# The low parts of a streamed weight matrix: all on VectorE, in quarters, and none on GpSimd in the second pass

## The chip, the cores and the metric

The kernel runs on one core of one Trainium2 chip. The metric is device time in microseconds (us). TensorE multiplies matrices, VectorE (DVE in the rows) and ScalarE (ACT) work element by element on 128 partitions, GpSimd (POOL) can do the same and issues the indirect DMAs here, and SyncE (SP) issues the plain DMAs. Each engine runs its own instructions in order and waits for others by semaphores. PE is TensorE's matmul, PEld its weight load.

## The reference

One decoder layer for 512 prompt tokens and 32 sample tokens (544 columns). What matters here is its last part, a channel mixer of 16384 single-neuron experts with a dense expansion in the kernel:

```
xt = rms_norm(h)                                   # n tokens x 1024
s1, s2 = scores of xt @ w_query against keys1, keys2      # 8 heads, 128 + 128 keys
top, idx = the 16 best of the 256 sums of the 16 best of each  # per token and head
g   = softmax(top)
act = gelu(einsum('nd,nhkd->nhk', xt, expert_u[idx]))
out = einsum('nhk,nhkd->nd', g * act, expert_v[idx])
```

`expert_u` and `expert_v` are 16384 x 1024 in fp32, 64 MB each. All is fp32. The kernel makes each product of fp32 operands from three products of parts: a high part (a rounded copy) and a low part (the rest, value minus high part).

## The kernel before, in words

The mixer runs over `expert_u` twice. A step is 256 of the 16384 experts (`STEPS` = 64 steps, a 1 MB piece of u and one of v each).

**Pass one** (steps 0 to 63) computes the activations of tokens 0 to 255 for every expert and stores them to device memory (`acts_sparse`). **Pass two** (steps 64 to 127 of u, each followed four steps later by its v piece) does the 288 other tokens densely: activations times gates, then the product with v. In the same pass the first 256 tokens get their output sparsely: for each of 256 (token tile, slot) pairs k, GpSimd fetches one activation per partition (`fetch_unit`, L651) and one 4 KB row of v per partition (`fetch_row`, L658), and VectorE adds row times share into an accumulator in PSUM (`add_row`, L1428). Six row buffers (`RING`) stand between the two: the fetch of row k+6 waits until row k is used.

**A slot** of pass two is one round of the loop `for slot in range(ENDS)` that every engine has. From slot 4 on TensorE does `up` for step 64+slot (48 matmuls of 288 columns, two halves j of 24), then `down` for v piece slot-4 (48 matmuls, two halves o). ScalarE rounds the next u piece (`high_u`, L924) and the next v piece (`high_v`, L969), applies gelu (L954), and rounds the activations (L976). VectorE does, in this order: the second half of the last `down` is added (`add_block`, L1458), `split_u` of the next step (L1451), about two rows, `gate_acts` (two L1470), `split_v` (L1485), `low_acts` (two L1479), the first half of this `down` is added (L1458), and about two rows. SyncE loads the next pieces when a low part has freed their buffer.

**Low parts of u.** `on_vector(t)` says who makes the low part of step t: in pass one GpSimd always; in pass two VectorE, but of the steps from 69 on every third (t = 69, 72, ... 126: 20 steps) GpSimd. GpSimd's `split_u` (L646) is two instructions of 1024 elements, each telling `u_lo_pool`. It stands in GpSimd's row of work between the first and second half of the slot's fetches. `wait_low_u` makes TensorE wait for whichever engine has the step. VectorE's `split_u` and `split_v` are one instruction of 2048 elements each. The low part of v is always VectorE's.

In pass one GpSimd does the 64 low parts of u, and that of step 64, as two instructions each.

Of the kernel before, what the change touches and what calls it, by code (L numbers as in the profile page):

```python
# [93 lines left out]

def on_vector(t):

    return t > STEPS and (t <= STEPS + BESIDE or t % 3 != 0)


def splits_until(t):  # L100
# [5 lines left out]
def u_buffer(t):  # L106

    return t % 3 if t < STEPS else 1 - t % 2
# [24 lines left out]
def rows_added_at(slot):  # L133

    return range(rows_until(slot), rows_until(slot + 1))
# [29 lines left out]
def build_layer(nc, io):  # L165
# [134 lines left out]
    def by_blocks(ap):  # L300

        return ap.rearrange("p (k c) -> p k c", k=KD)
# [176 lines left out]
    with nc.Block() as block:  # L479
# [118 lines left out]
        def _(pool):  # L598
# [42 lines left out]
            def split_u(t):  # L641
                pool.wait_ge(u_hi_done, t + 1)
                w = t % 2 if t < STEPS else place_of_u(t - STEPS)
                for j in range(2):
                    cols = slice(P * j, P * (j + 1))
                    pool.tensor_tensor(lows[w][:, :, cols], by_blocks(u_raw[u_buffer(t)])[:, :, cols],  # L646
                                       highs[w][:, :, cols].bitcast(F32), ALU.subtract).then_inc(u_lo_pool, 1)

            def fetch_unit(k):

# [28 lines left out]
            for slot in range(ENDS):  # L679
                for k in range(PIECE * slot, PIECE * slot + PIECE):  # L680
                    if k < AHEAD:
                        fetch_unit(k)
                mine = rows_added_at(slot)
                for k in mine[:len(mine) // 2]:
                    fetch_ahead(k)
                if slot + 1 < STEPS and not on_vector(STEPS + slot + 1):
                    split_u(STEPS + slot + 1)
                for k in mine[len(mine) // 2:]:
                    fetch_ahead(k)

        @block.scalar
# [323 lines left out]
        def _(v):  # L1015
# [432 lines left out]
            def split_u(t):  # L1448
                w = place_of_u(t - STEPS)
                v.wait_ge(u_hi_done, t + 1)  # L1450
                v.tensor_tensor(lows[w], by_blocks(u_raw[u_buffer(t)]), highs[w].bitcast(F32), ALU.subtract)\  # L1451
                    .then_inc(u_lo_vector, 2)

            def add_block(c, o):

# [26 lines left out]
            def split_v(c):  # L1482
                w = place_of_v(c)
                v.wait_ge(v_hi_done, c + 1)
                v.tensor_tensor(lows[w], by_blocks(v_raw[c % 2]), highs[w].bitcast(F32),  # L1485
                                ALU.subtract).then_inc(v_lo_done, 1)

            def add_total(tile):

# [491 lines left out]
```

## Time and profile before

| | |
|---|---|
| median of 3 runs | 2034.12 us (2033.16 to 2038.95) |
| the profiled execution | 2026.33 us |
| its span in the trace | 2024.9 us |
| pass two with both products, of the span | 1102 to 1991 us |
| TensorE matmul busy, of the span | 1847.7 us (91%) |
| VectorE, ScalarE, GpSimd busy | 1482.8, 822.7, 1199.6 us |

The profile's page gives shares over the whole program, which has stages with different limits. Pass one and the stages before it end near 1062 us, and the loop with both products, 60 slots, runs from 1102 to 1991 us. A row on a wait names the engine and line that waited and the one that released it. "issue" means that nothing the profile shows released it, and "remote" a releaser that it did not find.

### The profile page before, as it was taken

How to read it: one execution, taken by the hardware profiler on the slowest of the kernel's cores; microseconds unless marked ns; L12 is line 12 of the kernel's file. 1: busy time of each engine (PE TensorE's matmuls, PEld its weight loads, DVE VectorE, ACT ScalarE, POOL GpSimd, SP SyncE). 2: the span in 40 equal slices, each digit the busy share in tenths (PEclk: the TensorE clock that was granted, in tenths of full speed). 3: DMA queues.
4: the chain of work that ended last, by engine and by line, in shares of the span. 5: the costliest groups of instructions: out<-in, count | busy, mean ns of one | idle time of the engine just before them, and what ended most of it. 6: DMA issues, size and time to landing. Idle time of an engine off the chain costs nothing.

```text
span 2024.9 us, 37848 instructions
## 1 busy us (share of the span) xinstructions
PE 1847.7 (91%) x14571; PEld 1740.4 (86%) x14571; DVE 1482.8 (73%) x2584; ACT 822.7 (41%) x1103; POOL 1199.6 (59%) x855
## 2 busy tenths in 40 slices
PE   7988988798999999999997999998988998989798
PEld 6977764368999999999997999898988998989798
DVE  3669665523589889857765787888768788887977
ACT  4233764423214454457673333343333333333332
POOL 3322222232236888855647787878777778787861
PEclk8999999889999999999998999899999998998999
DMA  5434878652125777756778888988878998998875
GB/s 169 74 106 151 289 253 291 220 219 81 63 98 163 222 225 231 226 185 261 268 289 295 279 302 316 323 311 312 301 279 291 330 318 299 319 318 284 291 276 196
DMA packets 207789, 492.19 MB, mean 243 GB/s; under 512 B 34209, under 2 KB 119266, under 8 KB 187138
## 3 DMA queue, kind: packets, MB, share of 16 engines
q1 hardware_dynamic: 145906, 319.11, 46.4%
q0 software_dynamic: 55296, 167.94, 23.0%
q10 hardware_dynamic: 6416, 2.78, 1.0%
q8 instruction: 116, 1.90, 0.4%
q14 instruction: 55, 0.45, 0.1%
HBM read 449.10 MB, written 40.66 MB: 242 GB/s over the span
## 4 chain that ended last, share of the span: by engine, by line
PE 60%; POOL 13%; DVE 11%; issue 6%; ACT 4%; another core or an unknown queue 3%; DVEq 2%; DMA 1%; ACTq 0%; SPq 0%; POOLq 0%
PE pair L1529 16%; PE pair L1531 16%; PE pair L1530 16%; POOL v_rows L658 6%; POOL picked_a L651 6%; PE pair L1862 3%; PE pair L1674 3%; DVE pair L1428 2%; POOL w_lo L646 2%; DVE act L1470 1%; PE pair L1686 1%; DVEq L1422 1%; PE pair L1726 1%; PE pair L1812 1%
## 5 line engine op out<-in xcount | busy, mean ns | idle before, releaser
L1529 PE MATMUL pair<-x_hi,w_hi 128*128 128x256 f32 (+2 forms) x2224 | 664.9, 299 | 78.1 <-POOL w_lo L646 55.4
L1530 PE MATMUL pair<-x_lo,w_hi 128*128 128x256 f32 (+2 forms) x2224 | 653.8, 294 | 0.7 <-issue 0.7
L1531 PE MATMUL pair<-x_hi,w_lo 128*128 128x256 f32 (+2 forms) x2224 | 652.5, 293 | 0.1
L1529 PEld LDWEIGHTS pair<-x_hi,w_hi 128*128 128x128 f32 x2224 | 434.2, 195 | 83.4 <-POOL w_lo L646 58.8
L1530 PEld LDWEIGHTS pair<-x_lo,w_hi 128*128 128x128 f32 x2224 | 433.7, 195 | 1.9 <-issue 1.7
L1531 PEld LDWEIGHTS pair<-x_hi,w_lo 128*128 128x128 f32 x2224 | 431.9, 194 | 0.7 <-issue 0.7
L658 POOL DMA_INDIRECT v_rows<-in_v_t,at_row x256 | 294.5, 1150 | 148.6 <-DVE pair L1428 80.0
L651 POOL DMA_INDIRECT picked_a<-acts_sparse,at_unit x256 | 325.8, 1273 | 80.3 <-issue 74.9
L1428 DVE SCALAR_TENSOR_TENSOR pair<-v_rows,share,pair 128x1024 f32<-128x1024 f32 x254 | 327.5, 1289 | 25.2 <-issue 3.0
L646 POOL TENSOR_TENSOR w_lo<-w_raw,w_hi 128x1024 fp32r<-128x1024 f32 x106 | 253.1, 2410 | 90.6 <-ACT w_hi L924 90.4
L630 POOL TENSOR_TENSOR w_lo<-w_raw,w_hi 128x2048 fp32r<-128x2048 f32 x22 | 101.5, 4614 | 233.9 <-ACT w_hi L715 233.9
L1529 PE MATMUL pair<-a_hi,w_hi 128*128 128x288 f32 x688 | 209.3, 304 | 14.0 <-issue 13.3
L1530 PE MATMUL pair<-a_lo,w_hi 128*128 128x288 f32 x688 | 208.2, 303 | 6.9 <-issue 6.9
L1531 PE MATMUL pair<-a_hi,w_lo 128*128 128x288 f32 x688 | 208.7, 303 | 5.6 <-issue 5.5
L954 ACT ACTIVATE act<-pair 128x288 f32<-128x288 f32 x128 | 52.6, 411 | 365.7 <-PE pair L1531 198.1
L646 POOL TENSOR_TENSOR w_lo<-v_raw,w_hi 128x1024 fp32r<-128x1024 f32 x64 | 151.6, 2392 | 60.5 <-ACT w_hi L924 60.2
L924 ACT ACTIVATE w_hi<-w_raw 128x2048 fp32r<-128x2048 f32 x64 | 122.4, 1912 | 75.4 <-PE pair L1531 39.0
L1529 PEld LDWEIGHTS pair<-a_hi,w_hi 128*128 128x128 f32 x688 | 133.6, 194 | 15.8 <-issue 15.6
L1470 DVE TENSOR_TENSOR act<-act,g_in 128x288 f32<-128x288 f32 x128 | 77.4, 634 | 92.9 <-ACT act L954 67.1
L1530 PEld LDWEIGHTS pair<-a_lo,w_hi 128*128 128x128 f32 x688 | 133.9, 195 | 10.6 <-issue 10.6
L1531 PEld LDWEIGHTS pair<-a_hi,w_lo 128*128 128x128 f32 x688 | 133.7, 194 | 8.7 <-issue 8.5
L954 ACT ACTIVATE act_out<-pair 128x256 f32<-128x256 f32 x128 | 51.2, 401 | 137.8 <-PE pair L1531 126.4
(234 smaller groups left out, 3775.9 us busy)
## 6 DMA issues: line engine op xcount, KB each, us to landing
w_raw<-in_u_t SPq DMA_DIRECT2D x74, 1024.0 KB, 5.3
v_raw<-in_u_t SPq DMA_DIRECT2D x54, 1024.0 KB
w_raw<-in_v_t SPq DMA_DIRECT2D x128, 256.0 KB
v_raw<-in_v_t SPq DMA_DIRECT2D x128, 256.0 KB
gates<-g_out SPq DMA_DIRECT2D x9, 2048.0 KB, 8.6
g_in<-gates SPq DMA_DIRECT2D x16, 1152.0 KB
v_ring<-in_cache_v SPq DMA_DIRECT2D x64, 256.0 KB, 3.8
v_ring<-in_cache_v POOLq DMA_DIRECT2D x64, 256.0 KB, 4.6
```

The costliest lines, as they stand in the source:

```text
L630: pool.tensor_tensor(w_lo[:, chunk % 2, :], w_raw[:, chunk % 2, :], w_hi[:, chunk % 2, :].bitcast(F32), ALU.subtract).then_inc(w_split, 1)
L646: pool.tensor_tensor(lows[w][:, :, cols], by_blocks(u_raw[u_buffer(t)])[:, :, cols], highs[w][:, :, cols].bitcast(F32), ALU.subtract).then ...
L651: pool.indirect_dma_start(picked_a[:, k:k + 1], None, every_unit[:, :], bass.IndirectOffsetOnAxis(ap=at_unit[:, k:k + 1], axis=0))\
L658: pool.indirect_dma_start(v_rows[:, k % RING, :], None, every_row[:, :], bass.IndirectOffsetOnAxis(ap=at_row[:, k:k + 1], axis=0))\
L924: sc.activation(into, by_blocks(u_raw[u_buffer(t)]), ACT.Copy).then_inc(u_hi_done, 1)
L954: sc.activation(kept, made, ACT.Gelu).then_inc(gelu_done, 1)
L1428: v.scalar_tensor_tensor(total, row, share[:, k:k + 1], total, ALU.mult, ALU.add).then_inc(row_used, 1)
L1470: v.tensor_tensor(mine, mine, g_in[:, slot, :, GCHUNK * tile:GCHUNK * (tile + 1)], ALU.mult)\
L1529: te.matmul(out, s_hi, m_hi, start=start, stop=False)
L1530: te.matmul(out, s_hi, m_lo, start=False, stop=False)
L1531: return te.matmul(out, s_lo, m_hi, start=False, stop=stop)
L1674: last = te.transpose(bank(PAGE_TURN[j % 2])[:, P * pr:P * (pr + 1)], pages_in[chunk % 4][:, j, P * pr:P * (pr + 1)], ident[:, :])
```

## The change

`on_vector(t)` is true for every step of pass two, so the 20 low parts that GpSimd made are VectorE's, and GpSimd only fetches there. VectorE's instruction for a low part, of u and of v, is cut into four of 512 elements each, with one semaphore update behind the last. GpSimd's in pass one is cut in two again: four instructions of 512 elements, an update behind each second. GpSimd's loop of pass two keeps its order of fetches and loses the split between them (the `split_u` call stays in the text, but its condition is never true).

```diff
 def on_vector(t):
 
-    return t > STEPS and (t <= STEPS + BESIDE or t % 3 != 0)
+    return t > STEPS
...
                 for j in range(2):
                     cols = slice(P * j, P * (j + 1))
-                    pool.tensor_tensor(lows[w][:, :, cols], by_blocks(u_raw[u_buffer(t)])[:, :, cols],
-                                       highs[w][:, :, cols].bitcast(F32), ALU.subtract).then_inc(u_lo_pool, 1)
+                    for first in (0, KD // 2):
+                        mine = slice(first, first + KD // 2)
+                        last = pool.tensor_tensor(lows[w][:, mine, cols], by_blocks(u_raw[u_buffer(t)])[:, mine, cols],
+                                                  highs[w][:, mine, cols].bitcast(F32), ALU.subtract)
+                    last.then_inc(u_lo_pool, 1)
...
-                mine = rows_added_at(slot)
-                for k in mine[:len(mine) // 2]:
-                    fetch_ahead(k)
                 if slot + 1 < STEPS and not on_vector(STEPS + slot + 1):
                     split_u(STEPS + slot + 1)
-                for k in mine[len(mine) // 2:]:
+                for k in rows_added_at(slot):
                     fetch_ahead(k)
...
             def split_u(t):
                 w = place_of_u(t - STEPS)
                 v.wait_ge(u_hi_done, t + 1)
-                v.tensor_tensor(lows[w], by_blocks(u_raw[u_buffer(t)]), highs[w].bitcast(F32), ALU.subtract)\
-                    .then_inc(u_lo_vector, 2)
+                for q in range(4):
+                    mine = slice(2 * q, 2 * q + 2)
+                    last = v.tensor_tensor(lows[w][:, mine], by_blocks(u_raw[u_buffer(t)])[:, mine],
+                                           highs[w][:, mine].bitcast(F32), ALU.subtract)
+                last.then_inc(u_lo_vector, 2)
...
             def split_v(c):
                 w = place_of_v(c)
                 v.wait_ge(v_hi_done, c + 1)
-                v.tensor_tensor(lows[w], by_blocks(v_raw[c % 2]), highs[w].bitcast(F32),
-                                ALU.subtract).then_inc(v_lo_done, 1)
+                for q in range(4):
+                    mine = slice(2 * q, 2 * q + 2)
+                    last = v.tensor_tensor(lows[w][:, mine], by_blocks(v_raw[c % 2])[:, mine],
+                                           highs[w][:, mine].bitcast(F32), ALU.subtract)
+                last.then_inc(v_lo_done, 1)
```

How the work stands on VectorE before, in slots 4 and 5. Slot 4 has no split of u, slot 5 has one; `w_lo`, `x_lo` are two of the three places of low parts, `pair` is PSUM.

```order
L1428 SCALAR_TENSOR_TENSOR pair<-v_rows,share,pair 128x1024 x3
L1470 TENSOR_TENSOR act_129<-act_129,g_in 128x288 x2
L1485 TENSOR_TENSOR x_lo<-v_raw_119,x_hi 128x8x256
L1479 TENSOR_TENSOR a_lo_128<-act_129,a_hi_127 128x288 x2
L1458 TENSOR_TENSOR resid<-resid,pair 128x288
L1428 SCALAR_TENSOR_TENSOR pair<-v_rows,share,pair 128x1024 x2
L1458 TENSOR_TENSOR resid<-resid,pair 128x288
L1451 TENSOR_TENSOR w_lo<-w_raw,w_hi 128x2048
L1418 TENSOR_TENSOR share<-share,picked_a 128x8
L1428 SCALAR_TENSOR_TENSOR pair<-v_rows,share,pair 128x1024 x2
```

The same place in the changed kernel. The first row here is the last row of slot 3, then comes slot 4's own split of u (L1453, before L1451).

```order
L1428 SCALAR_TENSOR_TENSOR pair<-v_rows,share,pair 128x1024
L1453 TENSOR_TENSOR w_lo<-v_raw_115,w_hi 128x512 x4
L1428 SCALAR_TENSOR_TENSOR pair<-v_rows,share,pair 128x1024 x2
L1473 TENSOR_TENSOR act_129<-act_129,g_in 128x288 x2
L1490 TENSOR_TENSOR x_lo<-v_raw_119,x_hi 128x2x256 x4
L1482 TENSOR_TENSOR a_lo_128<-act_129,a_hi_127 128x288 x2
L1461 TENSOR_TENSOR resid<-resid,pair 128x288
L1428 SCALAR_TENSOR_TENSOR pair<-v_rows,share,pair 128x1024 x2
L1461 TENSOR_TENSOR resid<-resid,pair 128x288
L1453 TENSOR_TENSOR w_lo<-w_raw,w_hi 128x512 x4
```

Every slot now has a split of u, and each split is four instructions. Nothing else on VectorE moved.

GpSimd before, late in pass two, around one of its splits.

```order
L651 DMA picked_a<-acts_sparse,at_unit 128x1
L658 DMA v_rows<-in_v_t,at_row 128x1024
L646 TENSOR_TENSOR w_lo<-w_raw,w_hi 128x8x128 x2
L651 DMA picked_a<-acts_sparse,at_unit 128x1
L658 DMA v_rows<-in_v_t,at_row 128x1024
```

In the changed kernel the row L646 is gone there and the fetches follow each other without a break; from one of the old splits to the next there are 26 fetches, or 13 pairs, in three slots.

## Rows read from the trace of the kernel before

**Rows 1.** The page: busy time, and the span in 40 slices.

```profile
PE 1847.7 (91%) x14571; PEld 1740.4 (86%) x14571; DVE 1482.8 (73%) x2584; ACT 822.7 (41%) x1103; POOL 1199.6 (59%) x855
...
PEclk8999999889999999999998999899999998998999
DMA  5434878652125777756778888988878998998875
```

**Rows 2.** Stretches: us, busy (instructions) per engine, granted clock, DMA share, GB/s.

```profile
1102.00:1991.00 889.00, 805.72 (x5722) 792.72 (x5720) 723.79 (x736) 314.55 (x359) 678.90 (x522) 0.94 0.87 302
...
1573.00:1599.00 26.00, 26.00 (x198) 26.00 (x197) 21.73 (x24) 10.41 (x12) 20.82 (x18) 1.00 1.02 377
1651.00:1690.00 39.00, 38.45 (x290) 38.21 (x288) 37.78 (x41) 16.27 (x19) 28.62 (x23) 1.00 0.87 297
```

**Rows 3.** Waits of TensorE, 1102 to 1991: us in total, times, longest.

```profile
PE pair L1529 <- POOL w_lo L646: 51.9, 10, 8.7
PE pair L1529 <- issue: 14.7, 22, 1.5
PE pair L1530 <- issue: 8.3, 18, 1.0
PE pair L1531 <- issue: 5.9, 13, 1.1
PE pair L1890 <- issue: 2.1, 3, 1.1
```

**Rows 4.** GpSimd in order, 1546 to 1576: start, us, what, [idle before].

```profile
1553.46 1.00 POOL L651 DMA_INDIRECT picked_a<-acts_sparse,at_unit  x1 [0.30 <-issue]
1554.76 2.27 POOL L658 DMA_INDIRECT v_rows<-in_v_t,at_row  x1 [0.30 <-issue]
...
1562.04 4.67 POOL L646 TENSOR_TENSOR w_lo<-v_raw,w_hi 128x1024 fp32r<-128x1024 f32 x2
```

**Rows 5.** VectorE in order, 1546 to 1592.

```profile
1553.92 2.29 DVE L1485 TENSOR_TENSOR x_lo<-v_raw,x_hi 128x2048 fp32r<-128x2048 f32 x1
...
1563.97 4.89 DVE L1451 TENSOR_TENSOR w_lo<-w_raw,w_hi 128x2048 fp32r<-128x2048 f32 x1 [1.64 <-ACT w_hi L924]
...
1578.66 0.45 DVE L1458 TENSOR_TENSOR resid<-resid,pair 128x288 f32<-128x288 f32 x1
...
1588.45 2.29 DVE L1485 TENSOR_TENSOR w_lo<-v_raw,w_hi 128x2048 fp32r<-128x2048 f32 x1 [0.48 <-ACT w_hi L969]
1590.66 0.82 DVE L1479 TENSOR_TENSOR a_lo<-act,a_hi 128x288 fp32r<-128x288 f32 x2
1591.40 0.45 DVE L1458 TENSOR_TENSOR resid<-resid,pair 128x288 f32<-128x288 f32 x1
```

**Rows 6.** Groups by shape, 1102 to 1991: busy, mean ns, idle before.

```profile
L1428 DVE SCALAR_TENSOR_TENSOR pair<-v_rows,share,pair 128x1024 f32<-128x1024 f32 x245 | 315.9, 1289 | 24.0 <-issue 2.5
L651 POOL DMA_INDIRECT picked_a<-acts_sparse,at_unit x236 | 300.0, 1271 | 69.2 <-issue 69.2
L658 POOL DMA_INDIRECT v_rows<-in_v_t,at_row x246 | 283.2, 1151 | 139.2 <-DVE pair L1428 73.6 <-issue 65.4 <-DVE pair L1426 0.3
L1485 DVE TENSOR_TENSOR w_lo<-w_raw,w_hi 128x2048 fp32r<-128x2048 f32 x20 | 45.8, 2292 | 10.5 <-issue 5.4 <-ACT w_hi L969 5.0
```

**Rows 7.** The picks (L651) of the whole program: ns min/median/max.

```profile
L651 POOL DMA_INDIRECT picked_a<-acts_sparse,at_unit x256: 940/945/2990, 1061.9 to 1957.3; - x128
```

**Rows 8.** The low parts on GpSimd: ns min/median/max; one by shape.

```profile
L646 POOL TENSOR_TENSOR w_lo<-v_raw,w_hi x64: 2352/2395/2417, 599.4 to 1923.5; 128x1024 fp32r<-128x1024 f32 x64
L630 POOL TENSOR_TENSOR w_lo<-w_raw,w_hi 128x2048 fp32r<-128x2048 f32 x22 | 101.5, 4614 | 233.9 <-ACT w_hi L715 233.9
```

**Rows 9.** In order, 1590 to 1612: TensorE, ScalarE, GpSimd.

```profile
1598.39 0.30 PE L1529 MATMUL pair<-x_hi 128*128 128x288 f32 x1
1598.52 0.29 PE L1530 MATMUL pair<-x_lo,x_hi 128*128 128x288 f32 x1
1598.65 0.30 PE L1531 MATMUL pair<-x_hi,x_lo 128*128 128x288 f32 x1
1598.78 0.30 PE L1529 MATMUL pair<-a_hi,w_hi 128*128 128x288 f32 x1
...
1604.98 0.41 ACT L954 ACTIVATE act<-pair 128x288 f32<-128x288 f32 x1 [6.81 <-remote]
...
1602.82 4.71 POOL L646 TENSOR_TENSOR w_lo<-w_raw,w_hi 128x1024 fp32r<-128x1024 f32 x2
```

**Rows 10.** Waits in pass one, and in slots 0 to 3.

```profile
PE pair L1529 <- POOL w_lo L646: 3.5, 5, 0.7
...
PE pair L1529 <- DVE w_lo L1451: 6.9, 2, 4.9
```

## The prediction

> **What bounds the kernel now.** I read the page first, then the stretches, then the waits of TensorE, then the engines in order of time around one long wait. The page shows TensorE busy 91% of the span, GpSimd only 59% [rows 1]; such a share says little about one stage. Pass two with both products takes 889 us for 60 slots, or 14.8 us a slot, at a mean granted clock of 0.94 [rows 2]. A slot has 96 matmuls. At full clock they start 0.13 us apart (three steps take 0.39 us [rows 9], and 290 in 38.45 busy us are 0.133 each [rows 2]), so a slot could take 96 x 0.132 = 12.7 us, 60 slots 762 us. About 127 us are lost. The waits name part of them: 51.9 us in 10 waits for GpSimd's low part of u, and 14.7 + 8.3 + 5.9 + 2.1 = 31 us in short gaps put down to "issue" [rows 3]. The other 44 us are mostly matmuls at half clock behind such stops: a mean clock of 0.94 is 12% of the time at 1.2 instead of 2.4 GHz, worth at most 0.06 x 889 = 53 us.
>
> Why is GpSimd late? It is serial and nearly full. An issue takes 0.945 us undisturbed [rows 7] and is followed by 0.30 us before the next. A group of 236 picks has 300.0 us of busy time and 69.2 us of such pauses, 246 rows 283.2 and 65.4 [rows 6]: 718 us of 889, and 20 splits of 4.7 us [rows 4, 9] are 94 more. That is 91% before any wait for a used row buffer. And issues get stretched: the one at 1554.76 took 2.27 us, since VectorE's split ran from 1553.92 to 1556.21; it ended 0.82 us behind it [rows 4, 5]. Over all, the groups' means of 1271 and 1151 ns instead of 945 are (0.326 x 236) + (0.206 x 246) = 128 us of stretching [rows 6]. It goes the other way as well: VectorE's split of 2.29 us took 4.89 us at 1563.97, beside GpSimd's, which ran until 1566.71 [rows 4, 5].
>
> A second loss is less plain. At 1598.65 TensorE starts the last matmul of an `up`, yet ScalarE's gelu that waits for it starts at 1604.98, six us later, and only when GpSimd has stopped issuing fetches and begun its split at 1602.82 [rows 9]. The gaps called "issue" lie in such places. They look bound to long unbroken runs of fetches, which occur in the slots without a split of u on VectorE, one in three. I can show this as a coincidence only.
>
> **The change, part by part.**
>
> *The splits leave GpSimd.* 20 x 4.7 = 94 us of its time go, and with them the 51.9 us of waits [rows 3]. GpSimd then has 4.1 pairs a slot (246 rows in 60 slots [rows 6]), 8.2 x 1.245 = 10.2 us, and some stretching: it fits in 12.8 us. It does not need to catch up, and waits for used rows instead. What is late next? VectorE's low part of u is the first work of its slot and has most of a slot until `up` needs it. Behind the wait for `u_hi_done` the whole rest of VectorE's slot is queued, but ScalarE rounds u at the slot's start, and VectorE runs some us behind.
>
> *VectorE gets them, in quarters.* From 1578.66 to 1591.40 VectorE goes once around a slot with both splits: 12.74 us, less a wait of 0.48, is 12.26 us [rows 5]. It has four rows; 0.1 more at 1.3 us is 0.13, and half a share update less (it comes every eighth row and is in this slot) is about -0.08: 12.3 us. Now the quarters. From the split of 2048 elements to the next instruction are 2.21 us, of a 288-element one 0.37 us (two of them 0.74, 1590.66 to 1591.40) [rows 5]. The slope is 1.84 / 1760 = 1.045 ns an element, so 0.07 us are fixed per instruction. Two splits of four instead of one are six more instructions, 0.42 us. That makes 12.7 to 12.8 us a slot, in all 60 instead of 40 slots. The bounds for the fixed cost: nothing (12.3 us), or each quarter a whole duration, 2.29 - 1536 x 0.001045 = 0.685 us, in place of 0.60 (13.5 us). I take the 0.07, whose row is nearest. So VectorE comes up from 723.8 us busy [rows 2] to the level of TensorE.
>
> The page "VectorE: DVE Perf Modes" of the Trainium skill (The TRN2 errata) speaks against quarters: a small tile pays the fixed cost each time, 151 cycles for a tensor_tensor, or 691 ns at 512 elements; and by its section "The DRAIN you can't avoid" the next instruction does not start until the pipe is empty. By that rule a split takes 4 x 0.69 = 2.76 us. The trace agrees with the single duration (2.29 us at 2048), but there the next instruction starts 0.08 us before the end. That the starts follow at 0.60 us is what the sum uses; the rule's result is a rival below.
>
> *Stretching.* An issue caught by a split now waits for the end of a quarter, at most 0.6 us, instead of 2.2. If GpSimd gets in between two quarters, three splits in place of two per pair of slots still stretch less than before: about 0.3 us in the mean. Bounds: nothing saved (2.1 us a slot, 128 / 60, which GpSimd can bear: 12.3 us), or all. I take it as off the path. The reverse, a fetch holding up a quarter, would cost VectorE time that it has not: mean 2292 ns for 20 splits [rows 6] says that fetches did not hold up whole splits, and I count zero, up to 1 us a slot.
>
> The page "SBUF — State Buffer" of the Trainium skill (Who interferes with whom) has the port pair of VectorE and GpSimd as an exclusive lock for the whole instruction. By it a fetch that starts first would hold back a quarter as well. The trace shows the lock for the two splits (4.89 us) and for fetches that come second, not for fetches that come first.
>
> *Pass one and the start.* GpSimd's low parts of pass one are four instructions instead of two. 2048 elements in one take 4.61 us, two of 1024 take 2 x 2.395 = 4.79 [rows 8]: some 0.1 us per cut, 0.2 us a step. The cover is that GpSimd is ahead: TensorE waited 3.5 us in 5 waits [rows 10], so +1 us; without cover 65 x 0.2 = 13. In slots 0 to 3 TensorE waited twice for VectorE's split [rows 10], now 0.2 us longer each, +0.5.
>
> *DMA.* 889 us at 302 GB/s are 268 MB, 4.47 MB a slot [rows 2]. A slot of 13.3 us needs 336 GB/s. 26 us ran at 377 GB/s with TensorE fully busy [rows 2]: 11.9 us a slot. It is a tight third, not the bound.
>
> **The sum.** Slots can't be shorter than VectorE's 12.8 us (768 us). If only the waits for GpSimd go, with their share of half clock (44 x 52 / 83 = 28 us), and the "issue" bursts stay, it is 889 - 52 - 28 = 809 us, 13.5 us a slot. Between them the fullest stretch of VectorE in the profile decides: 37.78 of 39 us, 97% [rows 2]. 12.8 / 0.97 = 13.2 us; with three engines and the DMA all near their limit I take 13.3, so 798 us. 889 - 798 = 91 us, less 1.5, is 89.5 us. The profiled execution took 2026.33 us, 1.4 more than its span, so 1937. The median of the runs shown is 2034.12, 7.8 us above it; I carry that over: **1945 us**.
>
> **The rivals.**
>
> *The bursts stay* (0.18). The waits for GpSimd go, the 31 us of gaps and their 16 us of clock remain once in three slots. For it: I don't know their cause. Against: they come where VectorE had no split of u, and no such slot is left. 809 us: 2034 - 80 + 1.5 = 1956.
>
> *VectorE becomes the bound in full* (0.14). Quarters that don't overlap: 12.3 - 2 x 2.21 + 8 x 0.685 = 13.4 us, at 97% 13.9 us, 832 us: 1979. For it: VectorE has no slack, and each late signal that it waits for is lost. Against: the overlap of 0.08 us stands behind each instruction of [rows 5].
>
> *The wait passes to the DMA* (0.08). If only 320 GB/s can be held over the pass, a slot takes 14.0 us, 840 us: 1987. For it: DMA share 0.87 already [rows 2]. Against: 377 GB/s in full stretches.
>
> *Slower: late signals in every slot* (0.08). GpSimd now issues its 8.2 fetches with no split between; what broke its runs were stops of one to two us under VectorE's whole splits. If quarters no longer break them, a burst comes in each slot instead of each third. A burst costs (31 + 16) / 20 = 2.35 us; 60 x (12.8 + 2.35) = 909 us, 20 more than before: 2056. It turns slower where a burst a slot costs over 2.0 us. Against: waits for used rows break the runs too (73.6 us before [rows 6]).
>
> The forecast itself has 0.52.
>
> **Range and chances.** 80% range 1920 to 2000: its low end is near VectorE's own sum (889 - 768 = 121 less 1.5, or 1915), its high end takes in the DMA rival with 13 us beside it. The likeliest case alone: 1925 to 1965. A change of 0.3% (6 us) is about what a measurement of this kernel can tell. Faster needs a slot under 14.7 us: all cases but the last and a little of the two before: 0.90. Same 0.03, slower 0.07.
>
> **What would show it.** Right: waits of TensorE on w_lo L646 in pass two gone; slots of 13 to 13.5 us; mean clock there 0.97 or more; VectorE at 95% or more; four starts of a split 0.60 us apart; L651 and L658 means near 1.0 us; gelu starting right behind its matmul; DMA share above 0.93. Wrong: quarters at 0.69 us or longer from start to start (VectorE rival), "issue" gaps as many as before or thrice as many (burst rivals), waits of ScalarE's L924 and L969 on DMAs (DMA rival). If pass one gets longer by over 5 us, its cover was not there.

## The result, and the profile after

The changed kernel took 2014.89 us in the median of 4 runs (2005.37 to 2018.06), the kernel before, beside it, 2036.53 us. The ratio is 0.9886, 95% interval 0.9846 to 0.9926: by it some 23 us are gained, a quarter of the 89.5 forecast. The profiled execution took 2005.37 us, with a span of 2003.9.

The page of the changed kernel, against [rows 1] (its product lines are L1535 to L1537, `add_block` L1461, `split_u` L1453, `split_v` L1490, the fetches L654 and L661):

```profile
PE 1850.6 (92%) x14571; PEld 1734.5 (87%) x14571; DVE 1507.4 (75%) x2985; ACT 820.4 (41%) x1103; POOL 1008.7 (50%) x945
...
PEclk8999999789999999999998999999999999999999
DMA  4434878662124777766686998989988898988975
```

Pass two with both products, against [rows 2]:

```profile
1106.00:1990.00 884.00, 824.38 (x5867) 804.34 (x5866) 767.42 (x1142) 317.07 (x362) 477.53 (x483) 0.97 0.88 308
```

The granted clock rose from 0.94 to 0.97, GpSimd's busy time fell by 201 us in this stretch, and VectorE's rose. But VectorE was to be busy 95% and is at 767.42 / 884 = 87%, and the DMA share stayed at 0.88. Nothing is full. From the gelu of slot 4 to that of slot 63 it is 856.1 us, 14.51 a slot; before, 880.6 us, 14.92.

Waits of TensorE in that stretch, against [rows 3]:

```profile
PE pair L1537 <- issue: 20.4, 36, 1.6
PE pair L1535 <- issue: 19.8, 38, 1.7
PE pair L1536 <- issue: 17.8, 30, 1.7
PE pair L1535 <- DVE resid L1461: 0.5, 1, 0.5
```

The 51.9 us for GpSimd's low part are gone, as they had to be. In their place the gaps that no releaser explains grew from 31 to 58 us. One such place, in order of time, answers to [rows 4, 5, 9]. GpSimd first:

```profile
1432.03 0.94 POOL L661 DMA_INDIRECT v_rows<-in_v_t,at_row  x1 [1.99 <-DVE pair L1428]
1433.27 0.94 POOL L654 DMA_INDIRECT picked_a<-acts_sparse,at_unit  x1 [0.30 <-issue]
1434.52 0.94 POOL L661 DMA_INDIRECT v_rows<-in_v_t,at_row  x1 [0.30 <-issue]
...
1442.49 0.94 POOL L661 DMA_INDIRECT v_rows<-in_v_t,at_row  x1 [0.30 <-issue]
1443.74 1.03 POOL L654 DMA_INDIRECT picked_a<-acts_sparse,at_unit  x1 [0.31 <-issue]
1448.69 0.94 POOL L661 DMA_INDIRECT v_rows<-in_v_t,at_row  x1 [3.92 <-DVE pair L1428]
```

TensorE in the same stretch:

```profile
1438.73 0.29 PE L1537 MATMUL pair<-a_hi,w_lo 128*128 128x288 f32 x1
...
1441.44 0.29 PE L1537 MATMUL pair<-a_hi,w_lo 128*128 128x288 f32 x1 [0.33 <-issue]
1442.16 0.39 PE L1535 MATMUL pair<-a_hi,w_hi 128*128 128x288 f32 x1 [0.43 <-issue]
1443.60 0.29 PE L1536 MATMUL pair<-a_lo,w_hi 128*128 128x288 f32 x1 [1.04 <-issue]
1443.72 0.29 PE L1537 MATMUL pair<-a_hi,w_lo 128*128 128x288 f32 x1
1445.73 0.40 PE L1535 MATMUL pair<-a_hi,w_hi 128*128 128x288 f32 x1 [1.71 <-issue]
...
1446.65 0.44 PE L1537 MATMUL pair<-a_hi,w_lo 128*128 128x288 f32 x1
```

VectorE:

```profile
1434.79 2.49 DVE L1453 TENSOR_TENSOR x_lo<-w_raw,x_hi 128x512 fp32r<-128x512 f32 x4
...
1440.68 2.53 DVE L1490 TENSOR_TENSOR w_lo<-w_raw,w_hi 128x512 fp32r<-128x512 f32 x4
1443.14 0.81 DVE L1482 TENSOR_TENSOR a_lo<-act,a_hi 128x288 fp32r<-128x288 f32 x2
1446.59 0.45 DVE L1461 TENSOR_TENSOR resid<-resid,pair 128x288 f32<-128x288 f32 x1 [2.63 <-remote]
```

The last matmul of a `down` half is the first row: it ends at 1439.02. VectorE's `add_block`, which waits for it alone, stands free for 2.63 us and starts at 1446.59, 7.6 us behind that matmul. GpSimd issues ten fetches on end from 1432.03 to 1444.77; the signal comes 1.8 us after the last. The time is lost ahead of the semaphore's update, not behind it: the trace has that update at 1446.56, 0.02 us before `add_block` starts (as in 58 of the 64 late signals that are counted further below). Meanwhile TensorE runs 14 matmuls of the next half on at full pace, then creeps, and its last rows here are longer (0.44 us). I call this a late signal. The quarters themselves ran as forecast: four in 2.49 us.

The groups by shape, against [rows 6]:

```profile
L1428 DVE SCALAR_TENSOR_TENSOR pair<-v_rows,share,pair 128x1024 f32<-128x1024 f32 x252 | 324.8, 1289 | 23.1 <-issue 0.4
L661 POOL DMA_INDIRECT v_rows<-in_v_t,at_row x247 | 245.6, 994 | 319.1 <-DVE pair L1428 251.5 <-issue 67.6
L654 POOL DMA_INDIRECT picked_a<-acts_sparse,at_unit x236 | 231.9, 983 | 71.9 <-issue 71.9
L1490 DVE TENSOR_TENSOR w_lo<-v_raw,w_hi 128x512 fp32r<-128x512 f32 x84 | 52.6, 688 | 10.7 <-ACT w_hi L969 5.8 <-issue 4.8
```

An issue takes 0.98 to 0.99 us instead of 1.15 to 1.27. GpSimd is no longer behind: it waits 251.5 us for used rows, before 73.6. Of the 128 us of stretching some 21 are left ((0.049 x 247) + (0.038 x 236)).

### The profile page after: what moved, and what is told of

Its sections match the earlier page's. It is cut to its first block, busy times and chain, and to the rows that moved or that the text cites. A ratio compares the mean times of both kernels' runs of the same rounds, so it can differ in the third digit from the quotient of the medians.

```text
span 2003.9 us, 38296 instructions
## 1 busy us (share of the span) xinstructions
PE 1850.6 (92%) x14571; PEld 1734.5 (87%) x14571; DVE 1507.4 (75%) x2985; ACT 820.4 (41%) x1103; POOL 1008.7 (50%) x945
## 4 chain that ended last, share of the span: by engine, by line
PE 82%; DVE 7%; issue 5%; ACT 3%; DMA 1%; DVEq 1%; POOL 1%; ACTq 0%; SPq 0%; POOLq 0%
PE pair L1535 23%; PE pair L1537 23%; PE pair L1536 23%; PE pair L1868 3%; DVE conv L1078 3%; PE pair L1680 2%; PE pair L1692 1%; PE pair L1732 1%; PE pair L1818 1%; PE pair L1545 1%; PE pair L1645 1%; PE pair L1667 1%; ACT w_hi L924 1%; POOL w_lo L648 1%; ACT page_kt L826 1%
## 5 line engine op out<-in xcount | busy, mean ns | idle before, releaser
L1535 PE MATMUL pair<-x_hi,w_hi 128*128 128x256 f32 (+2 forms) x2224 | 655.9, 295 | 24.4 <-DVE x_lo L1034 13.7
L1537 PE MATMUL pair<-x_hi,w_lo 128*128 128x256 f32 (+2 forms) x2224 | 645.1, 290 | 5.2 <-issue 5.2
L1536 PE MATMUL pair<-x_lo,w_hi 128*128 128x256 f32 (+2 forms) x2224 | 646.8, 291 | 3.0 <-issue 2.9
L1535 PEld LDWEIGHTS pair<-x_hi,w_hi 128*128 128x128 f32 x2224 | 427.2, 192 | 29.3 <-issue 22.9
L1537 PEld LDWEIGHTS pair<-x_hi,w_lo 128*128 128x128 f32 x2224 | 425.2, 191 | 6.5 <-issue 6.4
L1536 PEld LDWEIGHTS pair<-x_lo,w_hi 128*128 128x128 f32 x2224 | 426.7, 192 | 3.2 <-issue 3.0
L661 POOL DMA_INDIRECT v_rows<-in_v_t,at_row x256 | 254.4, 994 | 333.6 <-DVE pair L1428 254.9
L654 POOL DMA_INDIRECT picked_a<-acts_sparse,at_unit x256 | 251.9, 984 | 82.9 <-issue 77.7
L648 POOL TENSOR_TENSOR w_lo<-w_raw,w_hi 128x512 fp32r<-128x512 f32 x172 | 216.6, 1292 | 78.9 <-ACT w_hi L924 78.9
L1537 PE MATMUL pair<-a_hi,w_lo 128*128 128x288 f32 x688 | 207.6, 302 | 12.5 <-issue 12.4
L1535 PE MATMUL pair<-a_hi,w_hi 128*128 128x288 f32 x688 | 207.6, 302 | 10.2 <-issue 10.0
L924 ACT ACTIVATE w_hi<-w_raw 128x2048 fp32r<-128x2048 f32 x64 | 122.3, 1912 | 71.7 <-PE pair L1537 50.3
L1537 PEld LDWEIGHTS pair<-a_hi,w_lo 128*128 128x128 f32 x688 | 132.4, 192 | 16.3 <-issue 16.3
L1535 PEld LDWEIGHTS pair<-a_hi,w_hi 128*128 128x128 f32 x688 | 131.8, 192 | 15.6 <-issue 15.2
L648 POOL TENSOR_TENSOR w_lo<-v_raw,w_hi 128x512 fp32r<-128x512 f32 x88 | 111.3, 1296 | 53.3 <-ACT w_hi L924 53.3
L924 ACT ACTIVATE w_hi<-v_raw 128x2048 fp32r<-128x2048 f32 x43 | 82.2, 1911 | 73.1 <-PE pair L1537 52.4
```

The lines of the kernel that those rows point to most:

```text
L648: last = pool.tensor_tensor(lows[w][:, mine, cols], by_blocks(u_raw[u_buffer(t)])[:, mine, cols], highs[w][:, mine, cols].bitcast(F32), AL ...
L654: pool.indirect_dma_start(picked_a[:, k:k + 1], None, every_unit[:, :], bass.IndirectOffsetOnAxis(ap=at_unit[:, k:k + 1], axis=0))\
L661: pool.indirect_dma_start(v_rows[:, k % RING, :], None, every_row[:, :], bass.IndirectOffsetOnAxis(ap=at_row[:, k:k + 1], axis=0))\
L924: sc.activation(into, by_blocks(u_raw[u_buffer(t)]), ACT.Copy).then_inc(u_hi_done, 1)
L1535: te.matmul(out, s_hi, m_hi, start=start, stop=False)
L1536: te.matmul(out, s_hi, m_lo, start=False, stop=False)
```

## The experiments

For reading them: the batches ran one after the other, and the kernel before took 2006 us in the first of them and 2029 to 2037 us in the four others and in the first comparison; so ratios are compared within a batch, and the first batch is taken by itself. The first two batches are on record with the same chip number, 1, the others with 15, 14 and 13. Words in capitals (RUNS, TRAFFIC, SITE, HOLD, PACE) are names of theories; the expectations say what each means.

### First batch: quarters and fetches, one at a time

**whole_splits**: the changed kernel with each of VectorE's splits in one instruction again.

```diff
-                for q in range(4):
-                    mine = slice(2 * q, 2 * q + 2)
-                    last = v.tensor_tensor(lows[w][:, mine], by_blocks(u_raw[u_buffer(t)])[:, mine],
-                                           highs[w][:, mine].bitcast(F32), ALU.subtract)
-                last.then_inc(u_lo_vector, 2)
+                v.tensor_tensor(lows[w], by_blocks(u_raw[u_buffer(t)]), highs[w].bitcast(F32), ALU.subtract)\
+                    .then_inc(u_lo_vector, 2)
```

> Changed kernel, but VectorE's splits are whole again (one instruction of 2048 elements); the steps' low parts are all VectorE's as in the changed kernel. TensorE's waits in pass two of the changed kernel are no longer for GpSimd but 65 us of short gaps put down to issue, with signals of TensorE that arrive one to seven us late. Theory RUNS: the late signals come from GpSimd issuing four and more fetches without a stop. A whole split stops GpSimd for up to 2.2 us, so runs are shorter: issue gaps under 45 us, time 1985 to 2000. Theory TRAFFIC: they come from the amount of DMA traffic, whoever issues it: gaps as in the changed kernel (55 to 75 us), time 2000 to 2015, at most 0.4 us a slot less for the instructions that go.

**before_quarters**: the kernel before with only VectorE's splits in quarters (the opposite edit of the same lines; GpSimd keeps its 20 low parts).

> Kernel before, with nothing but VectorE's splits in quarters; GpSimd keeps its 20 low parts of u. RUNS: quarters stop GpSimd less, so it is less late for its low parts (waits 52 us down to 20 to 40), but its unbroken runs get longer and issue gaps go from 31 to 50 us or more: 2030 to 2050. TRAFFIC: GpSimd is less late, and gaps stay near 31: 2005 to 2025.

**small_rows**: the changed kernel with 64 bytes of a row per partition fetched instead of 4096.

```diff
-                pool.indirect_dma_start(v_rows[:, k % RING, :], None, every_row[:, :],
+                pool.indirect_dma_start(v_rows[:, k % RING, 0:16], None, every_chunk[:, :],
```

> Changed kernel, but each fetched row of v is 64 bytes a partition instead of 4096 (the sums of tokens 0 to 255 are left out in effect; VectorE's work on the row buffers is unchanged, and a memset of them of some 6 us stands in GpSimd's pass one). GpSimd issues as many fetches as before, the traffic of the rows (2 MB a slot) is gone. RUNS: late signals and issue gaps stay, 50 to 75 us, time 2000 to 2015. TRAFFIC: gaps under 20 us, slots near 13 us, time 1930 to 1955.

**few_picks**: the changed kernel with only every eighth `fetch_unit` issued.

```diff
             def fetch_unit(k):
 
+                if k % PIECE:
+                    return
```

> Changed kernel, but only every eighth pick (the 4-byte fetch of an activation, L651 before) is issued, the others are left out; the traffic of the rows is whole. GpSimd issues 4.6 fetches a slot instead of 8.2 and stops after each second one. RUNS: late signals go, issue gaps under 25 us, time 1935 to 1960. TRAFFIC: a pick moves 512 bytes in all, so nothing changes: gaps 55 to 75 us, time 2000 to 2015.

| first batch | us | ratio to before, interval | "issue" gaps | us a slot |
|---|---|---|---|---|
| whole_splits | 1935.94 | 0.9664 (0.9641 to 0.9688) | 0 | 13.28 |
| before_quarters | 1974.91 | 0.986 (0.9837 to 0.9884) | 0 | 14.03 |
| small_rows | 1911.97 | 0.9542 (0.9524 to 0.9559) | 0 | 12.74 |
| few_picks | 1904.17 | 0.9503 (0.9483 to 0.9523) | 0 | 12.76 |

Slots here and below are gelu of slot 4 to gelu of slot 63 over 59, gaps TensorE's from 1100 to 1900 us. All were far faster than either theory said, and not one gap was put down to "issue", with quarters or whole. So the batch could not tell the theories apart; it showed that gaps depend on something beside the kernel. It also showed the quarters at work where no signal is late: before_quarters gained 31 us on the kernel before with no low part moved, and small_rows, with every quarter and all 8.1 fetches a slot, reached 12.74 us a slot. In before_quarters issues take 1.00 us in the mean, and TensorE still waited 49.3 us for GpSimd.

### Second batch: the same kernels again, and two weaker changes

**after_again** is the changed kernel and **before_again** the kernel before, unchanged.

> The changed kernel as it is, beside its variants. In the four kernels run last no gap of TensorE was put down to issue; the changed kernel's first trace had 65 us of them. RUNS (late signals come from unbroken runs of GpSimd's fetches, whatever else): 60 us or more of issue gaps again, ratio to before 0.985 to 0.993. SITE (late signals depend on where the program ran, the run of fetches is not enough): no such gaps, then the quarters and the fetches that sit between them are all that is left over whole splits, 1950 to 1975 us with before at 2006, ratio 0.972 to 0.985.

> The kernel before, for its trace beside the variants. RUNS: 25 to 35 us of issue gaps in pass two. SITE: under 5 us of them, and the waits for GpSimd's low part of u 45 to 55 us as before; the first product of pass two's down near 1102 us.

**broken_runs**: a memset of one column on GpSimd behind every second pair of fetches.

```diff
                 for k in rows_added_at(slot):
                     fetch_ahead(k)
+                    if k % 2:
+                        pool.memset(pause[:, :].bitcast(mybir.dt.bfloat16)[:, k // 2:k // 2 + 1], 0.0)
```

> The changed kernel with an own instruction of GpSimd, a memset of one column, behind every second pair of fetches. RUNS: no run longer than four fetches, so late signals go: no issue gaps, 25 to 60 us less than the changed kernel. SITE: the changed kernel has none here, so the memsets only add GpSimd time (128 of some 0.1 us and the wait for the port): within 5 us of the changed kernel.

**halves**: VectorE's splits in two instructions of 1024 elements.

```diff
-                for q in range(4):
-                    mine = slice(2 * q, 2 * q + 2)
+                for q in range(2):
+                    mine = slice(4 * q, 4 * q + 4)
```

> The changed kernel with VectorE's low parts in two instructions instead of four. Four of 0.60 us from start to start instead of one of 2.21 cost 0.2 us each split, two cost 0.07. If only that counts, 0.27 us a slot less, 16 us less than the changed kernel at most. If fetches that get in between the parts cost VectorE time, it lies between whole splits (1936 us with before at 2006) and the changed kernel, nearer to whole.

| second batch | us | ratio, interval | "issue" gaps | us a slot |
|---|---|---|---|---|
| after_again | 1986.67 | 0.9779 (0.9704 to 0.9855) | 47 | 14.23 |
| before_again | 2040.42 (one run) | | 24 | 15.07 |
| broken_runs | 1998.07 | 0.9815 (0.9745 to 0.9885) | 50 | 14.41 |
| halves | 2002.86 | 0.9848 (0.9749 to 0.9947) | 55 | 14.44 |

The gaps are back, in the changed kernel and in the one before. SITE holds in so far as something beside the kernel decides; but with the same chip number on record as in the first batch, the chip alone doesn't explain it. The memset changes nothing, and it is no test of RUNS: it takes 0.12 us and fits into the 0.30 us that stand between two fetches anyway (0.305 us in the median with it), so the fetches follow each other as before. Halves bring none of the gain of whole splits.

### Third batch: whole splits, bytes and fetches beside the changed kernel

The kernels are those of above; **after_3rd** is the changed kernel.

> The changed kernel for the third time, now beside whole splits on the same chip. With before near 2006 us and no issue gaps in before: SITE says 1940 to 1960 us and no issue gaps in the changed kernel either. With before near 2030: 1985 to 1995 us and 45 to 65 us of issue gaps, as in its second run.

> Whole splits again, beside the changed kernel on the same chip. HOLD (a whole split of 2.2 us on VectorE stops GpSimd's issues for so long that TensorE's signals get through; a quarter, or a memset of GpSimd's own, does not): ratio near 0.966 wherever it runs, under 20 us of issue gaps. SITE (only the place decides): where before has issue gaps it has 45 us or more of them too, and its ratio is within 0.005 of the changed kernel's.

> The changed kernel with rows of 64 bytes instead of 4096 per partition (its fetches are as many, their bytes a 64th), output not the reference's. TRAFFIC (late signals come from the bytes on the way): no issue gaps where the changed kernel has them, ratio 0.955. HOLD: as many issues as the changed kernel, so the gaps stay: 45 us or more.

> The changed kernel with every eighth fetch of an activation issued and the seven others left out (output not the reference's). GpSimd issues 4.7 fetches a slot instead of 8.2. HOLD: pauses between its issues are there, so the gaps of TensorE go, ratio 0.950. TRAFFIC: the picks are few bytes, so the gaps stay at 45 us or more and the ratio is 0.97 or above.

| third batch | us | ratio, interval | "issue" gaps | us a slot |
|---|---|---|---|---|
| after_3rd | 2020.7 | 0.9931 (0.9901 to 0.9961) | 60 | 14.62 |
| whole_splits_2nd | 1937.23 | 0.9494 (0.946 to 0.9529) | 17 | 13.30 |
| small_rows_2nd | 2029.71 | 0.9945 (0.9911 to 0.9978) | 60 | 14.75 |
| few_picks_2nd | 1903.34 | 0.9335 (0.9305 to 0.9366) | 0.3 | 12.77 |

This settles the main point. On one chip, with the same 8.1 fetches a slot, quarters take 83 us more than whole splits. Bytes are not the cause: a 64th of the rows' bytes leaves 60 us of gaps. Fewer fetches are a cure. Whole splits, in order of time; GpSimd:

```profile
1410.78 2.35 POOL L654 DMA_INDIRECT picked_a<-acts_sparse,at_unit  x1 [0.30 <-issue]
1413.43 0.95 POOL L661 DMA_INDIRECT v_rows<-in_v_t,at_row  x1 [0.30 <-issue]
1414.68 0.95 POOL L654 DMA_INDIRECT picked_a<-acts_sparse,at_unit  x1 [0.30 <-issue]
1415.94 2.88 POOL L661 DMA_INDIRECT v_rows<-in_v_t,at_row  x1 [0.31 <-issue]
```

and VectorE:

```profile
1410.02 2.28 DVE L1451 TENSOR_TENSOR x_lo<-w_raw,x_hi 128x2048 fp32r<-128x2048 f32 x1
...
1415.71 2.29 DVE L1485 TENSOR_TENSOR w_lo<-w_raw,w_hi 128x2048 fp32r<-128x2048 f32 x1
```

These two whole splits hold a fetch for 1.4 and 1.9 us over its 0.95; both holds end 0.82 or 0.83 us behind the split. Over the program 123 of 127 whole splits hold one so. GpSimd then has no slack: from slot 4 to slot 63 it issues, or pauses its 0.30 us, in all of the 785 us, and VectorE is the one to wait, 57.7 us for rows that have not landed. So it is GpSimd that sets the pace of whole splits, at 13.3 us a slot, and that costs less than the late signals do. TensorE's waits from 1106 to 1890 us:

```profile
PE pair L1529 <- issue: 16.8, 19, 2.3
PE pair L1529 <- DVE resid L1458: 5.7, 9, 1.1
```

These gaps stand at one line only, L1529, where in the changed kernel they are spread over all three product lines. In the first batch whole splits had 23.5 us of waits at this line, all put down to VectorE's L1458; here it is 22.5 us of both kinds, so most of the 17 us of "issue" may be that same wait. That is a reading, not shown.

### Fourth batch: how much, and where

**v_whole** has the low part of v whole and that of u in quarters, **u_whole** the reverse (the edit of whole_splits in one of the two functions). **half_picks** leaves out every second `fetch_unit` (`if k % 2: return`). **drained** adds a drain behind each fetch of a row:

```diff
                 if k + RING < ALL_ROWS:
                     fetch_row(k + RING)
+                    pool.drain()
```

> The changed kernel with the low part of v in one instruction, that of u in four. One whole split a slot holds up a fetch of GpSimd by over a us, where the changed kernel has none and whole splits have two. HOLD and PACE both expect something between: if the loss follows the number of holds, half of the changed kernel's issue gaps, 25 to 35 us, and 1970 to 1990 us where before is 2030 to 2036. If one hold a slot is enough to break the runs, under 10 us of gaps and about 1940.

> The other way round: u whole, v in four. Same expectation, 1970 to 1990 us and 25 to 35 us of gaps, or 1940 if one hold is enough. If it is not the number but the place (the split of v lies where the signals of the last up and the first down come), this one keeps more gaps than v_whole.

> The changed kernel with every second fetch of an activation left out (output not the reference's): 6.2 fetches a slot, between 8.2 (the changed kernel) and 4.7 (every eighth, no gaps). PACE (signals are late when fetches follow each other for long at 1.25 us): far fewer gaps, under 15 us, 1905 to 1940 us. Proportional to the number of fetches over 4.7: 25 us of gaps, 1950 to 1970.

> The changed kernel with a drain of GpSimd behind every fetch of a row; all fetches stay. If the drain makes GpSimd wait until the fetch's own descriptors are written, pairs are spaced out. PACE: the spacing of pairs grows from 2.5 us, gaps of TensorE go as with whole splits, 1930 to 1960 us. HOLD (only VectorE's holding of a fetch in progress helps) or a drain that costs nothing: as the changed kernel, 45 us of gaps or more, 1985 to 2020.

| fourth batch | us | ratio, interval | "issue" gaps | us a slot |
|---|---|---|---|---|
| v_whole | 1997.36 | 0.9806 (0.9753 to 0.9858) | 43 | 14.15 |
| u_whole | 1942.84 | 0.9553 (0.9509 to 0.9597) | 21 | 13.42 |
| half_picks | 1904.7 | 0.9354 (0.9316 to 0.9393) | 2 | 12.81 |
| drained | 2809.18 | 1.3788 (1.373 to 1.3846) | 0 | 27.47 |

The dose is not even: the whole split of u brings nearly all of the gain, that of v little. A part of this is that the two don't hold equally often: 60 of 63 whole splits of u held a fetch, but only 44 of 64 of v. half_picks is the cleanest row of the study. Every quarter is there and GpSimd's pauses come from left-out fetches alone. The changed kernel itself did not run in this batch or the next; that signals come late in this one is shown by v_whole's 43 us, and in both the kernel before took 2036 to 2037 us, not 2006. A stretch of it:

```profile
1400.00:1500.00 100.00, 99.92 (x752) 99.77 (x751) 97.22 (x148) 40.62 (x47) 51.00 (x50) 1.00 0.99 358
```

TensorE is busy without a break at full clock, the DMA runs at 358 GB/s, and VectorE is busy 97%: from slot 4 to slot 63 it has 1 us of waits over 0.15 us in 756, so 97% is what a VectorE without waits shows here. The drain is a poor probe. GpSimd in order:

```profile
1304.66 0.94 POOL L654 DMA_INDIRECT picked_a<-acts_sparse,at_unit  x1 [4.05 <-issue]
1305.90 1.44 POOL L661 DMA_INDIRECT v_rows<-in_v_t,at_row  x1 [0.30 <-issue]
1311.66 0.94 POOL L654 DMA_INDIRECT picked_a<-acts_sparse,at_unit  x1 [4.31 <-issue]
```

It waits 4 us and more behind nearly every pair, VectorE's rows come late, and TensorE waited 292.6 us for VectorE (L1462). No signal was late with fetches so far apart, but at 27.47 us a slot that says little on the question.

### Fifth batch: the same instructions, rows set apart

**spread_quarters**: VectorE's rows no longer come two by two, so that GpSimd, which waits for used rows, fetches in pairs with pauses. **spread_whole**: the same with whole splits.

```diff
-                    split_u(STEPS + slot + 1)
-                for k in mine[:len(mine) // 2]:
-                    add_row(k)
+                    split_u(STEPS + slot + 1, (0, 1))
+                add_some(0)
+                if u_split:
+                    split_u(STEPS + slot + 1, (2, 3))
                 for step in gated_at(slot):
                     gate_acts(step)
+                add_some(1)
                 if 0 <= c + 1 < STEPS:
-                    split_v(c + 1)
+                    split_v(c + 1, (0, 1, 2))
+                add_some(2)
+                if 0 <= c + 1 < STEPS:
+                    split_v(c + 1, (3,))
...
-                for k in mine[len(mine) // 2:]:
-                    add_row(k)
+                add_some(3)
```

> The changed kernel with the same instructions, but VectorE's four rows of a slot set apart: two quarters of u, a row, two quarters and the gates, a row, three quarters of v, a row, the last quarter, the low parts of the activations and a block, a row. GpSimd's fetch of a row waits for a used row, so pairs come some 3 us apart instead of four fetches on end at 1.25 us. PACE: no issue gaps to speak of (under 10 us) though VectorE never holds a fetch for long; 1905 to 1940 us where before is 2030 to 2037, ratio 0.935 to 0.955. HOLD: only whole splits help, 45 us of gaps or more, ratio 0.975 to 0.995.

> Whole splits with the rows set apart in the same way: split of u, a row, gates, a row, split of v, a row, activations and block, a row. Whole splits alone took 1937 us with no late signals in pass two; its losses there are waits for VectorE's sum into resid (9 to 24 us). Three instructions a split fewer than spread_quarters: PACE expects 1900 to 1940 us, at or under spread_quarters; HOLD expects it 50 us or more under spread_quarters.

| fifth batch | us | ratio, interval | "issue" gaps | us a slot |
|---|---|---|---|---|
| spread_quarters | 1957.6 | 0.9621 (0.9591 to 0.9651) | 23 | 13.63 |
| spread_whole | 1940.79 | 0.9538 (0.9507 to 0.9568) | 13 | 13.43 |

Spreading the rows alone, with no fetch and no quarter left out, has 23 us of gaps, where the changed kernel had 47 to 60 in its batches:

```profile
PE pair L1549 <- issue: 13.0, 25, 0.9
PE pair L1548 <- issue: 5.9, 11, 1.1
PE pair L1550 <- issue: 4.4, 11, 0.7
```

It lies between the two theories: the pause counts for a good part, not for all. With whole splits spreading brings nothing more (0.9538 against 0.9494 two batches before). The best that computes everything remains **whole_splits**: the change without its quarters on VectorE, 0.9494 of the kernel before and 83 us under the changed kernel on the same chip.

### What a late signal goes with

From each trace I took the signals of the last matmul of an `up` half to gelu and of a `down` half to `add_block`, from 1100 to 1900 us, where the receiver had been idle for over 0.15 us (so it waited for this). Late is a start over 0.4 us behind the matmul's end; otherwise it is 0.04. I counted the fetches begun in the 6 us before the end. Late of all, by that count:

```
                       0 to 2    3       4       5
changed kernel         0/29     8/23   39/48   17/17
after_again            0/30     6/25   34/46   14/14
after_3rd              0/33     5/25   42/50    5/5
small_rows_2nd         0/35     6/20   39/50   16/16
broken_runs            0/31     6/26   35/46    6/9
halves                 0/34     3/24   46/54   10/11
v_whole                0/23     7/36   33/43   17/17
u_whole                0/11     0/40   20/45   11/11
spread_quarters        0/10     1/15   24/88    7/7
spread_whole           0/1      1/55   16/51    5/5
whole_splits_2nd       0/1      1/32    5/28    3/3
half_picks             0/56     2/61     -       -
few_picks_2nd          0/76     0/4      -       -
kernel before          0/23     4/38   19/41   18/18
before_again           0/24     1/31   11/34   14/14
before_quarters, 1st batch  0/21  0/39  0/32   0/15
small_rows, 1st batch  0/10     0/39    0/34    0/2
whole_splits, 1st batch  0/1    0/29    0/31    0/2
```

With two or fewer fetches no signal is late, and with five 143 of 147 are, in all kernels but those of the first batch. At four it depends on how they lie: 74% to 84% in the changed kernel's three runs and with small rows, where they follow on end, 27% where they come in pairs, 18% where VectorE holds them. The count alone shows only that the two go together; that the density of fetches delays TensorE's signals is shown by the edits that changed it: few_picks_2nd beside the changed kernel on one chip, half_picks, and spread_quarters, which leaves nothing out. It takes something more that the first batch lacked, and by what path it acts is not shown.

## Why the prediction was wrong

The step that failed is the choice between forecast and last rival: "they come where VectorE had no split of u, and no such slot is left". With it late signals stood in the forecast's 13.3 us a slot at nothing. A slot took 14.51, and 1.2 us in each of 60 slots are 73 us, about the whole of the miss (2014.89 against 1945). The place was right in the main: of the "issue" gaps before, 25 of 30 us lay in the slots without a split of u on VectorE, though 15 of 41 late signals lay in others. The reading of it was wrong. It was not VectorE's split as such that kept signals in time, but that a whole one stops GpSimd in a fetch. The quarters took that away in every slot, and I had priced the lost stretching at zero or as a gain: "I take it as off the path". It was TensorE that it protected.

- *Waits for GpSimd, 51.9 us:* gone, right.
- *VectorE's slot of 12.8 us:* right. half_picks has every quarter and, free of late signals, 12.81 us a slot. Quarters start 0.60 us apart (four in 2.49 us), not 0.69. The VectorE rival falls. What the prediction took from the Trainium skill's page "VectorE: DVE Perf Modes" (The DRAIN you can't avoid) was half of the section: the next instruction does not start until the pipe is empty, but one that is not held starts earlier. The trace agrees with the second half: the starts here lie 0.08 us ahead of the ends.
- *Slot of 13.3 us, 798 us:* this is what whole splits gave (13.28 and 13.30), not what the change gave (14.51). 1945 us was forecast; whole splits took 1936 and 1937. That is luck: their pace was GpSimd's, not VectorE's, and where quarters had no late signals a slot took 12.8 us. The division by 0.97 counted something twice, since a VectorE without waits reads as 97% busy. (In the same way the VectorE rival's 13.4 us over 0.97 is 13.8, not 13.9, and VectorE has six splits in three slots where it had five, not three for two; neither decides anything.)
- *Stretching:* the size was right, issues at 0.98 to 0.99 us against a forecast "near 1.0". Its sign was not: GpSimd had no use for the time, and fetches came closer together.
- *Port lock* (the Trainium skill's page "SBUF — State Buffer", Who interferes with whom): a fetch that started first did not hold back a quarter. The 370 quarters of 508 that began while a fetch ran took 686 ns in the mean, the other 138 took 691. Between a fetch and VectorE's subtraction the trace shows the lock in one direction only; the same section has it that a `tensor_tensor` did not stall such DMAs, and here it does.
- *Clock:* 0.97 was reached, although the gaps grew.
- *Slower rival:* its mechanism came: late signals in 40 of 55 slots of the changed kernel, against 28 of 54 before. Its price was 2.35 us a burst and its turning point 2.0. Measured it is 14.51 - 12.81 = 1.70 us a slot, or 102 us in 60 slots; within the third batch, after_3rd against few_picks_2nd, it is 14.62 - 12.77 = 1.85. So the same mechanism left the change a gain of some 23 us. Price and turning point were close; the chance of 0.08 was too low for a cause that I could show "as a coincidence only".
- *DMA rival:* falls, half_picks held 358 GB/s.
- *Pass one:* cover was there; the first `down` began at 1107.2 instead of 1102.1, of which about 1 us is pass one and 4 us slots 0 to 3, where one signal was over 14 us late. GpSimd's quarters cost twice the forecast 0.2 us a step (4 x 1.293 = 5.17 us against 4.79 [rows 8]), and TensorE waited 4.1 us for them instead of 3.5 [rows 10]:

```profile
L648 POOL TENSOR_TENSOR w_lo<-w_raw,w_hi x172: 1267/1291/1340, 615.1 to 1056.5; 128x512 fp32r<-128x512 f32 x172
...
PE pair L1535 <- POOL w_lo L648: 4.1, 5, 0.9
```

What stays open. Why no signal was late in the first batch, where small_rows took 1912 us instead of 2030 with the same program; the changed kernel itself did not run there, so whether it would reach the forecast there is untried. Quarters without the move (before_quarters) ran only there, so what they cost the kernel before where signals come late is untried too. Why the whole split of u does most of the work: with it 28 signals of `up` and 3 of `down` are still late, with that of v 46 and 11, in the changed kernel 44 and 20; I have no run that moves it. And what TensorE and GpSimd share.

## What to carry to other kernels

An instruction that blocks another engine may be holding that engine off a third one: before cutting it up, ask who profits from the pause. When a profile has a stall that can be shown only as a coincidence, test or price it in the slots that the change makes alike, since the change may multiply it. And keep the two halves of a change apart: moving the low parts was worth 98 us here (whole_splits_2nd against the kernel before, third batch), and quartering VectorE's took 83 of these back.

## What the runs showed of the hardware

- TensorE's semaphore signals came mostly 1 to 8 us late (0.04 otherwise; 12.3 at the most in pass two's loop, in small_rows_2nd) where GpSimd had begun four or five indirect DMAs in 6 us, in every batch but the first. TensorE runs on for 14 matmuls (in the place shown), then has gaps of 0.3 to 1.7 us put down to "issue". The rows' bytes don't matter (64 or 4096 per partition: 60 us of gaps each).
- The same program took 1911.97 us in one batch and 2029.71 in another, with 0 and 60 us of such gaps. A comparison across batches can turn the sign: the changed kernel's 2020.7 us of the third batch beside the kernel before's 2006.23 of the first would read as slower.
- A GpSimd fetch that begins within VectorE's subtraction of two SBUF operands (2.28 us) is held and ends some 0.82 us behind it; one that began before it is not held (0.95 us in the median, whole splits), and does not hold it (2.28 us). In quarters the subtraction lets them through: 0.98 to 0.99 us in the mean.
- A drain behind an indirect DMA on GpSimd holds it until the DMA has landed: the next fetch began 0.83 us behind the landing in the median, after 4.1 us idle (up to 9.1).
